# Halving the tiles of a triangular inverse in a gated delta rule layer: 64x64 blocks, turned two heads at once

## The reference, cut to what matters

```python
kb = kc * bc[..., None]
a_mat = jnp.where(tril_strict, jnp.einsum('bhnid,bhnjd->bhnij', kb, kc) * decay, 0.0)
l_mat = a_mat + jnp.eye(CHUNK)
u = triangular_solve(l_mat, vc * bc[..., None], lower=True, unit_diagonal=True)
w = triangular_solve(l_mat, kb * jnp.exp(gc)[..., None], lower=True, unit_diagonal=True)
```

## Time and profile before

| | us |
|---|---|
| median of 3 runs | 1152.38 (1150.73 to 1155.16) |
| the profiled execution | 1154.81 |
| its span in the trace | 1153.0 |
| PE busy | 1116.3 (97%) |
| DVE busy | 639.5 (55%) |
| ACT busy | 467.3 (41%) |
| POOL busy | 488.4 (42%) |
| mean granted clock of PE | 0.993 of 2.4 GHz |

### The profile page before, as it was taken

How to read it: one execution, slowest core, us unless ns; L and a number is a source line. 1 busy time by engine, 2 the same in 40 slices (tenths; PEclk the granted TensorE clock), 3 DMA queues, 4 the chain that set the end, 5 groups by cost and what they waited for, 6 DMA issues and landing times.

```text
span 1153.0 us, 15332 instructions
## 1 busy us (share of the span) xinstructions
PE 1116.3 (97%) x5588; PEld 898.4 (78%) x5588; DVE 639.5 (55%) x1249; ACT 467.3 (41%) x786; POOL 488.4 (42%) x373
## 2 busy tenths in 40 slices
PE   7999999999999999999999989999999999999997
PEld 6777777777997777777777767878888888888886
DVE  4266888666764685777767856487433333310003
ACT  6354443465444345544425545435322322311124
POOL 5533323364251445233323315543655455454442
PEclk9999999989999999999999999999999999999999
DMA  8677565300330333444312212443333333322211
GB/s 178 148 174 149 131 137 136 103 28 1 119 101 1 96 114 105 138 147 147 128 38 73 74 37 82 147 128 83 109 93 89 109 83 99 109 87 95 109 38 73
DMA packets 114800, 116.33 MB, mean 101 GB/s; under 512 B 4817, under 2 KB 97191, under 8 KB 114740
## 3 DMA queue, kind: packets, MB, share of 16 engines
q1 hardware_dynamic: 99952, 88.68, 28.0%
q10 hardware_dynamic: 14212, 26.13, 7.0%
q0 software_dynamic: 576, 0.73, 0.2%
HBM read 113.41 MB, written 2.12 MB: 100 GB/s over the span
## 4 chain that ended last, share of the span: by engine, by line
PE 91%; DVE 4%; ACT 2%; DMA 1%; issue 1%; SPq 0%; POOL 0%; DVEq 0%; ACTq 0%; POOLq 0%
PE bank L684 25%; PE bank L686 24%; PE bank L685 24%; PE bank L874 2%; PE bank L900 2%; PE bank L881 2%; PE bank L1036 1%; PE bank L971 1%; DMA raw<-w_in 1%; PE bank L1051 1%; PE bank L822 1%; ACT whi L1299 1%; PE bank L721 0%; PE bank L929 0%; PE bank L940 0%
## 5 line engine op out<-in xcount | busy, mean ns | idle before, releaser
L480 POOL TENSOR_TENSOR wlo<-raw,whi 128x512 fp32r<-128x512 f32 x312 | 427.0, 1400 | 585.8 <-ACT whi L1299 585.8
L684 PE MATMUL bank<-h_hi,whi 128*128 128x512 f32 x952 | 383.1, 402 | 2.8 <-DVE att_gate L1959 1.4
L686 PE MATMUL bank<-h_hi,wlo 128*128 128x512 f32 x952 | 372.8, 392 | 0.0
L685 PE MATMUL bank<-h_lo,whi 128*128 128x512 f32 x952 | 372.8, 392 | 0.0
L684 PEld LDWEIGHTS bank<-h_hi,whi 128*128 128x128 f32 x952 | 180.4, 190 | 54.2 <-issue 14.8
L1299 ACT ACTIVATE whi<-raw 128x2048 fp32r<-128x2048 f32 (+1 forms) x79 | 150.3, 1902 | 167.8 <-PE bank L686 153.5
L686 PEld LDWEIGHTS bank<-h_hi,wlo 128*128 128x128 f32 x952 | 179.7, 189 | 38.7
L685 PEld LDWEIGHTS bank<-h_lo,whi 128*128 128x128 f32 x952 | 179.9, 189 | 35.9 <-issue 1.5
L1425 ACT ACTIVATE pT_a<-bank 128x256 f32<-128x256 f32 (+3 forms) x80 | 32.5, 406 | 185.0 <-PE bank L881 184.7
L1829 DVE SCALAR_TENSOR_TENSOR ada_acc<-ada_w,small,ada_acc 128x512 f32<-128x512 f32 x84 | 70.9, 844 | 1.3 <-DMA ada_w<-w_ada 1.0
L686 PE MATMUL bank<-ffn_hi,wlo 128*128 (+1 forms) x176 | 69.5, 395 | 0.0
(11 more groups left out here) (372 smaller groups left out, 1568.0 us busy)
## 6 DMA issues: line engine op xcount, KB each, us to landing
raw<-w_in SPq DMA_DIRECT2D x66, 512.0 KB, 5.8
ada_w<-w_ada ACTq DMA_DIRECT2D x96, 256.0 KB, 2.8
raw<-w_up SPq DMA_DIRECT2D x44, 512.0 KB, 4.6
raw<-w_down SPq DMA_DIRECT2D x22, 512.0 KB, 3.7
raw<-w_out SPq DMA_DIRECT2D x16, 512.0 KB, 4.5
x_tok<-x SPq DMA_DIRECT2D x4, 512.0 KB, 5.5
toe<-bias_rows SPq DMA_DIRECT2D x8, 256.0 KB, 13.3
raw<-w_branch_swa SPq DMA_DIRECT2D x4, 512.0 KB, 3.5
```

Source lines behind the costliest of these rows:

```text
L480: pool.tensor_tensor(wlo[s][:, c], raw[s][:, c], whi[s][:, c].bitcast(F32), ALU.subtract)\
L684: pe.matmul(ps, wh, h_hi, start=start, stop=False)
L685: pe.matmul(ps, wh, h_lo, start=False, stop=False)
L686: return pe.matmul(ps, wl, h_hi, start=False, stop=stop)
```

## The change

The masks of the first five levels shrink to 64 columns, the same for the upper and the lower 64 partitions. In levels 0 to 4 everything that is not zero lies in the two diagonal 64x64 blocks of each head, so prod1 and prod2 compute only these: two matmuls of 64 rows, 64 weight columns and 64 moving columns for each head, in opposite quarters of the array, both writing the same 64 columns of one bank. `X` is kept in a new layout: for two heads (2k, 2k+1) the four 64x64 blocks stand side by side in the 128x128 tile of head 2k. One transpose turns such a tile with both heads in it, so `back` has two transposes, and ACT takes the blocks to their places in XT with four copies of 64 partitions x 128 elements. The last level has one 64x64 block for each head, its mask becomes a plain copy, and its update changes only the upper right block of XT.

The order changes too: prod1(l+1, 0) is issued ahead of prod2(l, 3), and masked(l+1, 0) ahead of update(l, 3), so that the levels form one sequence. On ACT the Silu of `gate` moves to the end of level 0, the table load for the logarithm to the end of level 1, the two `hi` to the ends of levels 2 and 3, and the copies to `h_hi` between the copies of level 4. On POOL the multiplications by `gate` go ahead of the two `lo`.

```diff
-    for n in range(N_LVL):
-        c[:, C_LVL + n] = merge(2 << n)
+    for n in range(N_LVL - 1):
+        c[:, C_LVL + n, 0:64] = np.tile(merge(2 << n)[0:64, 0:64], (2, 1))
...
+        HALF = (slice(0, 64), slice(64, 128))
+        def blocks(ap):
+            return ap[:, 0:256].rearrange("p (h i) -> p h i", h=4)
...
+            pool.wait_ge(S["gate_silu"], 1)
+            for p in range(4):
+                pool.tensor_tensor(qk_att[:, p, :], qk_att[:, p, :], gate[:, p, :], ALU.mult).then_inc(S["att_mix"], 1)
             lo(N_S1)
             lo(N_S1 + 1)
-            pool.wait_ge(S["gate_silu"], 2)
-            for p in range(4):
-                pool.tensor_tensor(qk_att[:, p, :], qk_att[:, p, :], gate[:, p, :], ALU.mult).then_inc(S["att_mix"], 1)
...
-                for h in range(DN_H):
-                    mm = pe.matmul(bank[c % 2][:, h * P:(h + 1) * P], AT[:, c, h, :], X[:, c, h, :], start=True, stop=True)
+                for h, g in product(range(DN_H), range(2)):
+                    o = slice(h * 64, h * 64 + 64)
+                    if l < N_LVL - 1:
+                        mm = pe.matmul(bank[c % 2][HALF[g], o], AT[HALF[g], c, h, HALF[g]], X[HALF[g], c, h // 2 * 2, h % 2 * 64:h % 2 * 64 + 64], start=True, stop=True)
+                    elif g == 0:
+                        mm = pe.matmul(bank[c % 2][HALF[1], o], AT[HALF[0], c, h, HALF[1]], X[HALF[0], c, h // 2 * 2, h % 2 * 64:h % 2 * 64 + 64], start=True, stop=True)
...
-                        mm = pe.matmul(bank[2 + c % 2][:, h * P:(h + 1) * P], XT[:, c, h, :], P1[:, c, h, :], start=True, stop=True)
+                        for r in HALF:
+                            mm = pe.matmul(bank[2 + c % 2][r, o], XT[r, c, h, r], P1[r, c, h, 0:64], start=True, stop=True)
...
-                        mm = pe.matmul(bank[4 + c % 2][:, h * P:(h + 1) * P], P1[:, c, h, :], XT[:, c, h, :], start=True, stop=True)
+                        mm = pe.matmul(bank[4 + c % 2][HALF[0], o], P1[HALF[1], c, h, 0:64], XT[HALF[1], c, h, HALF[1]], start=True, stop=True)
...
-                for h in range(DN_H):
-                    mm = pe.transpose(bank[4 + c % 2][:, h * P:(h + 1) * P], X[:, c, h, :], ident)
+                for k in range(2):
+                    mm = pe.transpose(bank[4 + c % 2][:, k * P:(k + 1) * P], X[:, c, 2 * k, :], ident)
...
             for l in range(N_LVL):
-                if l >= 1:
-                    prod1(l, 0)
                 for c in range(TT):
                     if c + 1 < TT:
                         prod1(l, c + 1)
+                    elif l + 1 < N_LVL:
+                        prod1(l + 1, 0)
...
-                    act.activation(XT[:, c], four(bank[4 + c % 2][:, :]), ACT.Copy).then_inc(S["dn_xtc"], 1)
+                    for (q, b), r in product(enumerate(HALF), HALF):
+                        ins = act.activation(XT[r, c, q::2, r], bank[4 + c % 2][b, 0:256].rearrange("p (k i) -> p k i", k=2)[:, :, r], ACT.Copy)
+                    ins.then_inc(S["dn_xtc"], 1)
...
+                    if l == 4:
+                        act.wait_ge(S["att_mix"], c + 1)
+                        act.activation(hh[:, 4 + c, :], qk_att[:, c, :], ACT.Copy).then_inc(S["att_hi"], 1)
-                if l in (1, 2):
-                    hi(N_S1 + l - 1)
+                if l == 0:
+                    evac(act, 32)
+                    act.activation(gate[:, :, :], gate[:, :, :], ACT.Silu).then_inc(S["gate_silu"], 1)
                 if l == 1:
                     act.activation(zs[:, :, :], zs[:, :, :], ACT.Silu).then_inc(S["gate_silu"], 1)
-                if l == 3:
-                    evac(act, 32)
-                    act.activation(gate[:, :, :], gate[:, :, :], ACT.Silu).then_inc(S["gate_silu"], 1)
-            for p in range(4):
-                act.wait_ge(S["att_mix"], p + 1)
-                act.activation(hh[:, 4 + p, :], qk_att[:, p, :], ACT.Copy).then_inc(S["att_hi"], 1)
-            act.preload_act_table_set("natural_log_exp_and_others")
+                    act.preload_act_table_set("natural_log_exp_and_others")
+                if l in (2, 3):
+                    hi(N_S1 + l - 2)
...
-                dve.tensor_copy(X[:, c], four(bank[4][:, :])).then_inc(S["dn_x"], 1)
+                for r in HALF:
+                    ins = dve.tensor_copy(X[r, c, 0::2, :].rearrange("p k (q i) -> p k q i", q=2),
+                                          four(bank[4][r, :])[:, :, r].rearrange("p (k q) i -> p k q i", q=2))
+                ins.then_inc(S["dn_x"], 1)
...
-                dve.tensor_tensor(P1[:, c], four(bank[c % 2][:, :]), each(m(C_LVL + l)), ALU.mult).then_inc(S["dn_p1s"], 1)
+                if l < N_LVL - 1:
+                    ins = dve.tensor_tensor(P1[:, c, :, 0:64], blocks(bank[c % 2]), each(m(C_LVL + l)[:, 0:64], 64), ALU.mult)
+                else:
+                    ins = dve.tensor_copy(P1[HALF[1], c, :, 0:64], blocks(bank[c % 2][HALF[1], :]))
+                ins.then_inc(S["dn_p1s"], 1)
...
-                    dve.tensor_tensor(X[:, c], X[:, c], four(bank[2 + c % 2][:, :]), ALU.subtract).then_inc(S["dn_upd"], 1)
+                    dve.tensor_tensor(X[:, c, 0::2, :], X[:, c, 0::2, :], bank[2 + c % 2][:, 0:256].rearrange("p (k i) -> p k i", k=2), ALU.subtract).then_inc(S["dn_upd"], 1)
                 else:
-                    dve.tensor_tensor(XT[:, c], XT[:, c], four(bank[4 + c % 2][:, :]), ALU.subtract).then_inc(S["dn_upd"], 1)
+                    off = XT[HALF[0], c, :, HALF[1]]
+                    dve.tensor_tensor(off, off, blocks(bank[4 + c % 2][HALF[0], :]), ALU.subtract).then_inc(S["dn_upd"], 1)
+            masked(0, 0)
             for l in range(N_LVL):
-                masked(l, 0)
                 for c in range(TT):
                     if c + 1 < TT:
                         masked(l, c + 1)
+                    elif l + 1 < N_LVL:
+                        masked(l + 1, 0)
```

More of the change, by code:

```diff
@@ L286, in turned, with each @@
             return ap.rearrange("p (h i) -> p h i", h=4)[:, :, ::-1]
-        def each(ap):
-            return ap.rearrange("p (o i) -> p o i", o=1).to_broadcast([P, 4, P])
+        def each(ap, n=P):
+            return ap.rearrange("p (o i) -> p o i", o=1).to_broadcast([P, 4, n])
+        HALF = (slice(0, 64), slice(64, 128))
+        def blocks(ap):
+            return ap[:, 0:256].rearrange("p (h i) -> p h i", h=4)
         class Signals(dict):
@@ L2060, in _ @@
             dve.wait_ge(S["dn_u"], 4)
-            dve.wait_ge(S["gate_silu"], 1)
+            dve.wait_ge(S["gate_silu"], 2)
             for c in range(TT + 2):
```

1 line of the change is left out of this document (added).

## The result

| | before | after |
|---|---|---|
| median | 1153.84 us (5 runs, 1150.73 to 1155.16) | 1145.17 us (5 runs, 1144.63 to 1147.42) |
| ratio | | 0.9933 [0.9915, 0.9951] |
| span of the profiled execution | 1153.0 | 1143.4 |
| mean granted clock | 0.993 | 0.988 |

The change is 8.7 us faster, where 17 were forecast. The range of 1130 to 1149 holds the result, but the size is off by half.

A forecast was written before the change was run, and what follows sets the result against it. TensorE, busy 97% of the span, was taken as the bound. The inverse's 56.4 us become 32.9 of work plus 5.5 of waits, 38.4; less 0.2 and 0.8, 17 us gained: 1135.4 us, range 1130 to 1149.

The forecast's parts named there:

- The products: Two 64x64 quarters per head on TensorE work beside each other: 0.45 us a product instead of 0.89.
- The first rival: Quarters of a product take turns on TensorE: product stays 0.89, step 2.30, 1.4 us gained, 1151 us; chance 0.13.
- The changes of size and the turn: TensorE per step: 0.3 us lost between quarter and full size (ends 0 and 0.4); two transposes, 0.22 for 0.44.
- VectorE: Masked product and update at 0.42 us each, at most 1.3 per step, hidden just below TensorE's 1.42.
- ScalarE's copies: Four copies of 64 x 128 for one of 512 elements: 0.9 us, ends 0.6 and 1.14, hidden behind TensorE.
- the pauses: ScalarE's work at level ends: 3.2 us after levels 0 and 1 costs TensorE 1.2, twice; 1.9 costs nothing.
- the last level's first wait: Block 0's second product waits for block 2's copy to leave its bank, behind the `h_hi` copies: 1.2 us.
- the rival: Low clock through the whole stage: its 32.9 us of work become 66, 13 us slower, 1166; chance 0.07.
- unevenness: Some 0.8 us taken off the gain for unevenness further on in the kernel.
- dear end of 42.5: Stage length in us at the unfavourable ends: copies 1.14, product 0.5; favourable end 34.8; together 1131 to 1139.
- one sequence: Next level's first product and mask ahead of this level's last second product and update; no wait counted for level ends.
- Queues: POOL's gate products and splits and SP's load of block 19 finish in time; the reordering costs nothing.

The follow-up runs named there:

- the filling: Thirteen idle matmuls ahead of the last level's second products: on the changed kernel 1142.74 us, on the changed kernel with its turn in quarter matmuls 1140.87 us.
- the banks: Changed kernel with the last level's second products in PSUM banks of their own and the `h_hi` copies behind level 4: 1139.69 us, ratio 0.9887.
- half the copies: Changed kernel without the two of ScalarE's four copies per block that cross between partition halves: 1138.35 us, ratio 0.9863.
- the weight loads: 512 KB loads held until level 1's copies: all, on the changed kernel with quarter-matmul turns, 1142.64 us; only the second of four, on the last version, 1139.93 us.
- last version: Changed kernel with turns in quarter matmuls, `h_hi` copies behind level 4, U/W of two blocks woven into the last level, own banks there: 1137.5 us, ratio 0.9863.

## Why the prediction was right in kind and wrong in size

**The products, right.** Forecast 0.45 beside each other, with 0.89 as the other end. Measured 0.47 alone and 0.52 with the change of size. The rule of the Trainium skill on row tiles and one bank ("TensorEngine Tiling (Array Packing)", "Restrictions and Gotchas") would have made it 0.89; for two diagonal quarters, which differ in their partitions of the bank as well as in their rows, these rows show no taking of turns. The first rival falls with it.

**The changes of size and the turn, right.** 0.3 and 0.22 forecast, 0.29 and 0.22 measured; the step 1.42 against 1.45. The work of the stage at full clock is 38.5 us busy less half of the 9.3 busy at clock 0.50 (3.40 + 5.91), an estimated 33.9, for 32.9 forecast.

**VectorE, right.** 0.42 for each operation, and TensorE waited for it hardly at all.

**ScalarE's copies, the first step that failed.** The step said: "I take 0.9; ends 0.6 and 1.14". Measured: 1.12, the dear end, which the earlier trace rows had shown for four copies of 128 elements. Halving the partitions takes nothing off: 0.272 for 64 x 128 against 0.278 for 128 x 128. With 1.12 the pauses cost 1.70 and 1.94 where 1.2 was forecast for each, there is another 0.59 after the second split, where the prediction had a pause of 1.9 at nothing, and the last level's first wait is 2.59 for the forecast 1.2. All of TensorE's idle time in the stage is 46.70 - 38.54 = 8.2 us for 5.5: 2.7 of the miss, and 7.0 of the 8.2 are waits for these copies. The Trainium skill, "ScalarE: Activation LUTs", "What `ACT_TABLE_LOAD` costs", gives back-to-back instructions an overlap of about 93 ns; by that the four would be an estimated 4 x 0.272 - 3 x 0.093 = 0.81. The timeline's 1.12 for four of 0.27 shows none of it here.

**The clock, the second and larger one.** The sum took it as 1.00, and the rival had it low through the whole stage, 13 us slower, and stopped at that: a price for all, and none for a part. Its reason, "the scan, idle for a tenth, kept 1.00", compared shares of idle time; the stage had 17% and single waits of 1.7 to 2.6 us. What happened is the part. The work at 0.50 in the stage cost half of 9.3, an estimated 4.7 us (by the step of quarters at the low clock, 310.48 to 313.00, 2.52 for 1.45, it is 4.0), and U and W 2.6 more: 7.3 us together. With 2.7 of waits and 1.0 of work this is 11.0; against it stand the 2.8 us of the earlier start and behind W, mostly luck as said above, and the 0.8 that the sum had held back for unevenness. 17 less 11.0 plus 3.6 is 9.6, the difference of the spans. Without the clock's 4.7 the stage would have taken 42.0, inside the forecast's own dear end of 42.5, which had the copies at 1.14; the prediction doesn't show how it came to its two ends. The clock is the term that carried the stage out of it.

That the wait in the last level is needed for the fall there is shown: the filling took the low clock out of the last level and of U and W twice, and the banks took the wait out and the low clock with it. That a wait is enough isn't shown. A stop of 1.72 us and one of 2.89 between quarters left the clock at 1.00, and whether the same waits between full size products would bring it down no run tests; so the small tiles may well have a part in it. The two terms hang together through TensorE's waits for ScalarE's copies: half the copies gave 6.8 of the 10.9 us that stage and U/W were over their forecast (57.4 for 38.4 + 8.1), and the banks with `h_hi` moved gave 8.6. What isn't settled is when exactly a wait does it. After the wait of 1.70 that ended at 300.88 the clock stayed up in the changed kernel, and after the like one that ended at 299.37 in the kernel with other banks it was low from 300.5 to 303.9. With half of the copies it fell in the last level after a wait of only 0.95.

**The last level's wait was seen, and not questioned.** "The second product of block 0 waits until the copy of block 2 has left its bank" stands in the prediction, as a price of 1.2. It measured 2.6, and with `h_hi` moved, where it was still 1.3 and 0.7, other banks took off 5.8 us in all.

**The order, underrated.** The prediction gave one sequence no figure of its own and counted its gain among the waits it left out. Alone, with full tiles, it is 2.4 us of the stage.

**Queues, right as far as semaphores go.** No wait of TensorE in the stage is put down to POOL, SP or a transfer. The stop of 0.55 us of "issue" is of the kind discussed with the weight loads.

## What to carry to other kernels

Price short instructions by the nearest row of a whole series of them (here four in 1.14), not by elements: on ScalarE, a piece with a quarter of the columns and half of the partitions costs nearly half of the whole (0.272 for 0.595). When the bound engine is made faster by a third, work out every follower's time per step against the new step, its pauses too, and give the clock a price for a part of the stage beside its waits. And look for waits that are only a choice of bank: here one pair of free banks gave up to 5.8 us, nearly as much as half of the copies (6.8), and at no cost in work.

## What the runs showed that was not expected

- Sixteen records of two diagonal quarters, 64 rows, 64 weight columns and 64 moving columns each, take 0.47 us, 29 ns a record, while writing the same columns of one bank.
- A copy of 64 x 128 from PSUM by ScalarE is 272 ns, one of 128 x 256 is 380, and several small ones in a row don't overlap (0.28 each).
- Matmuls that write nothing of use, some 3.0 us of them, shortened two stages by 3.5 us, since the clock stayed at 1.00 (one execution of each).
- When nearly all of TensorE's instructions are quarters it comes to stops of 0.2 to 2.9 us for which no semaphore is the cause, the long ones at the places of bulk loads. The clock stayed at 1.00 through one of 2.89 us. The changed kernel itself has one of 0.55 us.
- A gain of 16.8 us in the stages (last version) arrives as 15.2 in the medians, and one of 15.4 (banks in the changed kernel) as 13.0: low stretches of the clock elsewhere differ from kernel to kernel, and the four executions of the banks kernel alone lie 5.7 us apart. A total therefore says little about a change of 2 to 4 us.
